# A feed-forward's second matrix by Strassen's method for the latent tokens, with the context's products after them

## The reference

```python
def _ffn_sublayer(x, shift, scale, gate, w13, w2, g, b):
    a = _modulate(x, shift, scale) @ w13               # w13: 1024 x 5632, w2: 2816 x 1024
    y = (silu(a[..., :D_FF]) * a[..., D_FF:]) @ w2
    return _layer_norm(ALPHA * x + 0.5 * gate * y, g, b)

mod = silu(c) @ w_ada + b_ada                          # nine rows of 1024, for latent and context
x_lat = _ffn_sublayer(x_lat, ml[0:3], first weights)
x_ctx = _ffn_sublayer(x_ctx, mc[0:3], first weights)
y_lat = token_mixer(modulated x_lat, modulated x_ctx)  # two-way mLSTM, windowed attention
x_lat = _layer_norm(ALPHA * x_lat + ml[5] * y_lat)
x_lat = _ffn_sublayer(x_lat, ml[6:9], second weights)
```

## Time and profile before

| | |
|---|---|
| times of three runs | 2237.27, 2233.45, 2234.02 us (median 2234.02) |
| the profiled execution | 2234.15 us, of which the span is 2232.0 us |
| mean granted clock of TensorE | 0.993 of full speed |
| busy: PE, VectorE (DVE), ScalarE (ACT), GpSimd (POOL) | 98%, 65%, 38%, 7% of the span |
| transfers | 293 MB, a mean of 131 GB/s |
| chain of waits that ended last | PE 86%, VectorE 7%, ScalarE 3%, issue 2%, DMA 2% |

### The profile page before, as it was taken

How to read it: one execution, slowest core, us unless ns; L and a number is a source line. 1 busy time by engine, 2 the same in 40 slices (tenths; PEclk the granted TensorE clock), 3 DMA queues, 4 the chain that set the end, 5 groups by cost and what they waited for, 6 DMA issues and landing times.

```text
span 2232.0 us, 31733 instructions
## 1 busy us (share of the span) xinstructions
PE 2186.0 (98%) x11907; PEld 1859.5 (83%) x11911; DVE 1440.1 (65%) x2394; ACT 859.1 (38%) x1477; POOL 146.4 (7%) x153
## 2 busy tenths in 40 slices
PE   9999999999999999999999999989999999999997
PEld 6888888888888888799789978878778888887886
DVE  4677776676446355775562265765777777767787
ACT  3622222222233324542444427741633233326444
POOL 0000000000000000250010003520000000000001
PEclk8999999999999999999999999999999999999999
DMA  7144344553274537323230002432243443439772
GB/s 284 41 143 129 113 118 137 155 160 118 70 275 154 191 109 216 104 71 120 78 109 25 20 20 75 126 124 64 81 137 118 137 131 119 147 105 313 279 233 103
DMA packets 237933, 293.06 MB, mean 131 GB/s; under 512 B 16694, under 2 KB 164846, under 8 KB 237806
## 3 DMA queue, kind: packets, MB, share of 16 engines
q1 hardware_dynamic: 226766, 282.81, 40.0%
q10 hardware_dynamic: 11040, 8.52, 1.3%
HBM read 233.48 MB, written 57.80 MB: 131 GB/s over the span
## 4 chain that ended last, share of the span: by engine, by line
PE 86%; DVE 7%; ACT 3%; issue 2%; DMA 2%; POOL 0%; SPq 0%; ACTq 0%; DVEq 0%; POOLq 0%
PE psum L1278 11%; PE psum L1279 11%; PE psum L1280 11%; PE psum L617 4%; PE psum L619 4%; PE psum L618 4%; PE psum L1919 3%; PE psum L1920 3%; PE psum L1921 3%; PE psum L1444 2%; PE psum L2349 2%; PE psum L1445 2%; PE psum L1446 2%; PE psum L2897 2%; PE psum L1298 2%
## 5 line engine op out<-in xcount | busy, mean ns | idle before, releaser
L1278 PE MATMUL psum<-x_mix_h,x_op_h 128*128 128x512 f32 x640 | 249.9, 390 | 3.7 <-DVE v_sum L1098 3.7
L1279 PE MATMUL psum<-x_mix_l,x_op_h 128*128 128x512 f32 x640 | 249.5, 390 | 0.0
L1280 PE MATMUL psum<-x_mix_h,x_op_l 128*128 128x512 f32 x640 | 249.0, 389 | 0.0
L983 ACT ACTIVATE x_op_h<-raw 128x512 fp32r<-128x512 f32 x140 | 85.9, 627 | 207.3 <-PE psum L1280 121.9
L983 ACT ACTIVATE x_op_h<-w_sum 128x512 fp32r<-128x512 f32 x160 | 97.2, 624 | 160.5 <-DVE w_sum L961 96.0
L1278 PEld LDWEIGHTS psum<-x_mix_h,x_op_h 128*128 128x128 f32 x640 | 120.3, 188 | 28.4 <-DVE x_op_l L989 2.8
L1280 PEld LDWEIGHTS psum<-x_mix_h,x_op_l 128*128 128x128 f32 x640 | 120.2, 188 | 25.3
L1279 PEld LDWEIGHTS psum<-x_mix_l,x_op_h 128*128 128x128 f32 x640 | 120.3, 188 | 23.4
L1444 PE MATMUL psum<-s_high 128*128 128x512 f32 x308 | 120.4, 391 | 3.5 <-DVE s_low L1431 3.4
L1445 PE MATMUL psum<-s_low,s_high 128*128 128x512 f32 x308 | 119.9, 389 | 0.0
L1446 PE MATMUL psum<-s_high,s_low 128*128 128x512 f32 x308 | 119.8, 389 | 0.0
(11 more groups left out here) (411 smaller groups left out, 5702.3 us busy)
## 6 DMA issues: line engine op xcount, KB each, us to landing
raw<-in_ffn_w SPq DMA_DIRECT2D x154, 512.0 KB, 5.1
ada_slice<-in_w_ada SPq DMA_DIRECT2D x56, 512.0 KB, 3.7
f_terms<-g_half SPq DMA_DIRECT2D x77, 256.0 KB, 2.1
s_raw<-f_terms SPq DMA_DIRECT2D x77, 256.0 KB, 3.4
s_raw<-in_ffn_w SPq DMA_DIRECT2D x77, 256.0 KB, 4.1
f_rows<-g_out SPq DMA_DIRECT2D x44, 256.0 KB, 2.7
p_raw<-in_w_in SPq DMA_DIRECT2D x22, 512.0 KB, 5.1
early<-in_w_ada SPq DMA_DIRECT2D x16, 512.0 KB, 7.2
```

Source lines behind the costliest of these rows:

```text
L983: nc.scalar.activation(op_tiles(F, op)[0][:], OP_SOURCE[op], ACT.Copy).then_inc(F.hi, 1)
L1278: nc.tensor.matmul(o, wh[:, k], high(k), start=i < 4 and k == 0, stop=False, skip_group_check=i > 3)
L1279: nc.tensor.matmul(o, wh[:, k], low(k), start=False, stop=False, skip_group_check=i > 3)
L1280: last = nc.tensor.matmul(o, wl[:, k], high(k), start=False, stop=k == KH - 1, skip_group_check=i > 3)
```

## The change

1. The first feed-forward's gated rows become g_half1 as in the second: term stores to DRAM (`term_sp`), and the rows of the context stored alone (`ctx_store`). The four sums of halves of a pair are made by GpSimd (`quick1_pool`). Blocks 0 and 1 gate the odd block's halves in PSUM banks 7 and 6, and ScalarE copies them (`first_halves_act`).
2. The second matrix of the first feed-forward runs through the class `Second` (S1, 77 steps) for the latent tokens. Then come 11 pairs for the two tiles of the context (`c_loads_sp`, `c_high`, `c_low`, `c_unit`, `c_pe`, `c_evacuate_dve`), in banks 4 to 7, with the turns of latent tokens 512 to 1023 behind the first four pairs. The gate rows move into the last quick block.
3. `T2`'s order is latent tokens 512 to 1023, 0 to 511, context. The first 14 projection groups are kv for tiles 4 to 7, o for tiles 4 to 7, kv for 0 to 3, kv for the context, o for 0 to 3. GpSimd's x1 rows go in the order 4 to 7, 0 to 3.
4. The residual rows of the latent tokens are loaded behind pieces 16 to 23, those of the context after the last split of its weights. The rope loads move behind the first of these two.
5. The modulation slices have 512 columns: 112 of 256 KB, turned in 20 groups of four.

`second_loads`, `second_high`, `second_low`, `second_unit`, `second_pe`, `evacuate_dve`, `store_rows`, `plain_stored` and `quick_stored` are gone. Two lists of waits for a free place in the ring (`ring_free1`, `ring_free2`) and counts of what S1 has used before are passed to `Second`; the second feed-forward's order of work stays the same.

The core of the diff (lines of removed functions that are printed above, and buffer places, are left out):

```diff
+        def term_rest_pool(pool, F, pair):
+            e1, e2, o1, o2 = F.half
+            made = 4 * (pair + F.terms_before)
+            gated_in_place(pool, F, pair, 1, 1)
+            pool.wait_ge(term_made, made + 1)
+            nc.gpsimd.tensor_tensor(e2, e2, o2, ALU.add).then_inc(term_made, 1)
+            term_kept(pool, F, pair, 0, 2)
+            nc.gpsimd.tensor_tensor(e1, o2, e1, ALU.subtract).then_inc(term_made, 1)
+            pool.wait_ge(term_made, made + 3)
+            term_kept(pool, F, pair, 2, 1)
+            nc.gpsimd.tensor_tensor(o1, o1, e1, ALU.subtract).then_inc(term_made, 1)
...
+        def c_loads_sp(sp, S, f):
+            F, r = S.F, C_RAW[f]
...
+            if f < 4:
+                sp.wait_ge(F.y_added, 24)
+            else:
+                sp.wait_ge(F.lo, c_item(F, f - 4, 1) + 1)
+            sp.dma_start(c_raw[r][:], w2_view[F.which][f * P:(f + 1) * P, :]).then_inc(step_in[r], 16)
+            sp.dma_start(c_rows[f % 4][:], F.rows[f * P:(f + 1) * P, :]).then_inc(step_in[r], 16)
+        def c_high(act, S, p):
...
+            if p < 2:
+                act.wait_ge(F.lo, S.split(STEPS2 - 1))
+                act.wait_ge(F.y_added, 24)
+            elif p < 4:
+                act.wait_ge(F.y_ready, 4 * len(TERMS))
+            else:
+                act.wait_ge(F.pair_done, C_PARTS + max(i for i in range(p) if C_W2[i] == C_W2[p]) + 1)
+            if p >= 2:
+                act.wait_ge(F.pair_done, C_PARTS + p - 1)
...
+                c_in_place(act, S, f)
+                nc.scalar.activation(c_w2[C_W2[p]][0][:, i], c_raw[C_RAW[f]][:], ACT.Copy).then_inc(F.hi, 1)
...
+                h, l = [g[p % 2][:, i, t * P:(t + 1) * P] for g in (c_g_h, c_g_l)]
+                first, last = p == 0 and i == 0, p == PAIRS - 1 and i == 1
+                nc.tensor.matmul(o, h, wh[:, i, cols], start=first, stop=False)
+                nc.tensor.matmul(o, h, wl[:, i, cols], start=False, stop=False)
+                done = nc.tensor.matmul(o, l, wh[:, i, cols], start=False, stop=last)
...
+        def c_pe(pe, F, after_pair):
+            for p in range(PAIRS):
+                pe.wait_ge(F.lo, c_item(F, 2 * p + 1, 1) + 1)
+                if p == 0:
+                    pe.wait_ge(F.y_read, 12)
+                for u in range(4):
+                    done = c_unit(pe, p, u)
+                    if p == PAIRS - 1:
+                        done.then_inc(F.y_ready, 1)
+                if p < PAIRS - 1:
+                    done.then_inc(F.pair_done, 1)
+                after_pair(p)
...
+        SLICE_PLAN = [[2 * s + i for s in plan for i in range(2)] for plan in SLICE_PLAN]
+        MOD_UNITS = [(g, h, v) for g in range(MODS_LATE) for h in range(2) for v in range(VECTORS[g])]
         def slices_at(j, place):
-            return SLICE_PLAN[j][place:place + 1 if place < 2 else None]
...
+        def first_halves_act(act):
+            act.wait_ge(F1.glu_ready, F1.items.index((1, 1)) + 1)
+            act.wait_ge(F1.ab_ready, 2 * F1.n)
+            for n in range(2):
+                nc.scalar.activation(F1.half[2 + n], psum[:, 7 - n, :], ACT.Copy).then_inc(first_quarter, 1)
...
         def quick1_sp(sp):
...
             slice_sp(sp, 1)
             loaded = 2
             for j in range(QUICK):
+                pair, odd = j // 2 + 1, j % 2
                 if j < QUICK - 1:
                     quick_weights(sp, F, j)
+                if odd:
+                    term_sp(sp, F, pair, "S3")
                 else:
-                    second_loads(sp, F, 0)
-                if j:
-                    quick_stored(sp, F, j - 1, 1)
+                    for term in ("A22", "S1", "S2", "S4"):
+                        term_sp(sp, F, pair - 1, term)
                 if j == QUICK - 1:
-                    second_loads(sp, F, 1)
+                    for s in range(4):
+                        pieces_sp(sp, S1, s)
                 ahead = sum(len(p) for p in SLICE_PLAN[:j + 1])
-                for s in range(loaded, min(ahead + 1, len(SLICES))):
+                for s in range(loaded, ahead):
                     slice_sp(sp, s)
-                    loaded = s + 1
-                quick_stored(sp, F, j, 0)
-                quick_stored(sp, F, j, 2)
+                loaded = max(loaded, ahead)
+                term_sp(sp, F, pair, "A12" if odd else "A11")
+                ctx_store(sp, F, j + 2)
                 for s in range(loaded, min(ahead + 2, len(SLICES))):
                     slice_sp(sp, s)
                     loaded = s + 1
-            quick_stored(sp, F, QUICK - 1, 1)
+            for term in ("A22", "S1", "S2", "S4"):
+                term_sp(sp, F, PAIRS - 1, term)
...
+        def quick1_pool(pool):
+            term_first_pool(pool, F1, 0)
+            for pair in range(PAIRS - 1):
+                term_rest_pool(pool, F1, pair)
+                term_first_pool(pool, F1, pair + 1)
+            term_rest_pool(pool, F1, PAIRS - 1)
...
+        def second1_sp(sp):
+            S, F = S1, F1
+            for s in range(4, STEPS2):
+                pieces_sp(sp, S, s)
+                if 5 <= s < 5 + PAIRS:
+                    kept_sp(sp, S, s - 5)
+                if 16 <= s < 16 + TL:
+                    sp.dma_start(y[:, s - 16, :], token_rows(s - 16)).then_inc(rows_back, 16)
+            for f in range(FB):
+                c_loads_sp(sp, S, f)
+                if f == 17:
+                    kv_loads_sp(sp)
+            sp.wait_ge(F.lo, c_item(F, FB - 1, 1) + 1)
+            sp.dma_start(y[:, TL, :], token_rows(TL)).then_inc(rows_back, 16)
+            rope_loads_sp(sp)
+            piece_load(sp, 2)
+            piece_load(sp, 3)
+            sp.wait_ge(F.pair_done, C_PARTS + PAIRS - 1)
+            sp.dma_start(y[:, TL + 1, :], token_rows(TL + 1)).then_inc(rows_back, 16)
...
+            c_high(act, S, 0)
+            c_high(act, S, 1)
+            for i in range(4, TL):
+                norm_act(act, N1, i, ROWS1[i])
+            for p in range(2, PAIRS):
+                if p == PAIRS - 1:
+                    proj_high(act, 0)
+                    gates_high(act)
+                c_high(act, S, p)
+                if 2 <= p < 6:
+                    turned1_act(act, (2 * p - 4, 2 * p - 3))
+            proj_high(act, 1)
+            norm_act(act, N1, 8, ROWS1[8])
+            norm_act(act, N1, 9, ROWS1[9])
...
+                add_part_dve(dve, S, 2, t)
+            c_low(dve, S, 0)
+            for t in range(4):
+                gate_part_dve(dve, S, 3, t)
+                add_part_dve(dve, S, 3, t)
+                dve.wait_ge(F.y_added, 36 + t + 1)
+                norm_sums_dve(dve, N1, 4 + t, ROWS1[4 + t])
+                if t == 1:
+                    c_low(dve, S, 1)
+            for p in range(2, PAIRS):
+                if p == PAIRS - 1:
+                    proj_low(dve, 0)
+                    gates_low(dve)
+                c_low(dve, S, p)
+                if p == 2:
+                    dve.wait_ge(F.pair_done, C_PARTS + 2)
+                if 2 <= p < 6:
+                    turned1_dve(dve, (2 * p - 4, 2 * p - 3))
+            dve.wait_ge(rows_back, 16 * TA)
+            for t in range(TC):
+                c_evacuate_dve(dve, F, t)
+            norm_sums_dve(dve, N1, TL, ROWS1[TL])
+            proj_low(dve, 1)
+            norm_sums_dve(dve, N1, TL + 1, ROWS1[TL + 1])
...
                     pe.wait_ge(N1.gates_kept, 4)
-                if u >= 2:
-                    pe.wait_ge(F1.y_read, u - 1)
...
+            def after_pair(p):
+                if p == 0:
+                    pe.wait_ge(F.y_read, C_READ)
+                if p < 4:
+                    for k in (2 * p, 2 * p + 1):
                         turn_pe(pe, T2, T2_BANKS, normed, (0, k))
-            second_pe(pe, F1, 0, first_free, gates)
-            second_pe(pe, F1, 1, second_free)
-            second_pe(pe, F1, 2, third_free, after_unit=turned)
-            for k in range(2):
-                turn_pe(pe, T2, T2_BANKS, normed, (1, k))
+            strassen_pe(pe, S, first_free)
...
-            out = rows(0, (TL, TL + 1, 0, 1, 2, 3)) + rows(1, range(4)) + rows(0, range(4, TL)) + rows(1, range(4, TL))
+            out = rows(0, range(4, TL)) + rows(1, range(4, TL)) + rows(0, range(4)) + rows(0, range(TL, TA)) + rows(1, range(4))
...
+        T2_BEFORE = {1: [(1, 0)], 2: [(1, 1)], 3: [(1, 2), (1, 3)], 4: [(1, 4)], 5: [(1, 5)], 6: [(1, 6)], 7: [(1, 7)],
+                     8: [(2, 0), (2, 1)], 9: [(2, 2), (2, 3)], 10: [(2, 4), (2, 5)], 11: [(2, 6), (2, 7)]}
+        T2_CHUNK = [1] * 4 + [0] * 4 + [2] * 2
...
         def kv_loads_sp(sp):
-            sp.wait_ge(F1.ab_ready, F1.products)
...
             sp.dma_start(gate_bias, b_gates[0:1, :].to_broadcast([P, 16])).then_inc(gate_in, 16)
-            wait_pair(sp, F1, 0)
+        def rope_loads_sp(sp):
+            sp.wait_ge(F1.lo, c_item(F1, FB - 1, 0) + 1)
             for t in range(TL):
```

(50 more changed lines are left out.)

616 lines of the change are left out of this document (286 added, 330 removed).

## The result

The kernel after takes 2238.46 us (median of 11 runs, 2235.46 to 2241.63) where before takes 2234.02 in the same runs: a ratio of 1.0022 with a 95% interval of 1.0014 to 1.0030. It is 0.2% slower; the forecast was 2232.1, a hair faster. The measured time lies inside the 2225 to 2240 that the forecast gave its own case, but on the side to which it gave a chance of 0.06 (0.27 for slower by any road). The profiled execution took 2239.72 us, 1.3 above the median; its span is 2237.5.

The account below looks back on a forecast made before the run. The prediction took PE, busy 98% of the span, as the bound. From 2234.15 us, +4.2 for the blocks, -23.6 for the second matrix's stage (132 fewer matmuls included) and +17.3 for the junction gave 2232.1 us; whole range 2209 to 2247.

Parts of the forecast that it names:

- its own case: Whole kernel: the saving is nearly all given back, 2232.1 us, own range 2225 to 2240; chance 0.42.
- stage of the second matrix: First feed-forward's second matrix, Strassen steps, context and gate rows: 283.4 us against 307.0, so -23.6, bounds -28 and -15.
- junction: From the last context product to the end of the first 14 projection groups: +17.3 us, bounds +3 and +25.
- rest: The part behind the fourteenth projection group; no change forecast, 0.
- Section 4: Junction: a late row load, late VectorE and GpSimd's x1 work blocking VectorE make it end at E+74; +17.3 us.
- Section 2: Blocks of the first matrix: GpSimd's 44 sums delay VectorE, mostly hidden in slack; +4.2 us, bounds 0 and 15.
- the late row: Junction's start: the last row tile lands at E+4.4, the context's evacuation waits for it, and PE stands 5 us.
- 1.5 for a clock that falls in the waits: Junction's end: 1.5 us added because PE's clock falls in the waits, giving E+74; mean clock near 0.9.
- VectorE's work too, in halves: Blocks of the first matrix: VectorE's work on the modulation slices stays the same, only in halves; no cost.
- Rival C: Blocks: GpSimd's three sums reach PE before v_sum's sixth product in every even block; 15 us, total 2243; chance 0.22.
- the fifth piece's wait: Start of the Strassen steps: the fifth piece is issued 2.3 us later as GpSimd makes three sums; +2.3 us.
- Rival B: Junction stays cheap, groups take 57 to 62 us, as VectorE gets in between GpSimd's operations; total 2216; chance 0.33.

Follow-up runs that it names:

- run 6: The kernel after, with the four sums of gated halves of each pair made by VectorE in the quick blocks, none by GpSimd; ratio 1.0008 to the kernel before.
- run 7: The kernel after, with each of the twenty modulation transposes one place later in its block; ratio 0.9998 to the kernel before.
- run 8: The kernel after, with the edits of run 6 and run 7 together; ratio 0.9994 to the kernel before.
- run 1: The kernel after, with GpSimd's x1 multiplications and additions cut to 8 columns, a measurement and no usable version; ratio 0.9953 to the kernel before.
- run 5: The kernel after, with the last row tile of y loaded ahead of the rope tables and two weight pieces; ratio 1.0002 to the kernel before.

## Why the prediction was wrong, by its own steps

The forecast's sum was -2.1 us, the medians differ by +4.4. Against the mean of the two profiles on each side (the gate rows, 3.6 us, are counted with the stage as in the forecast):

| part | before | after | difference | forecast |
|---|---|---|---|---|
| up to the stage | 621.3, 618.05 | 630.1, 628.3 | 9.5 - 3.6 = +5.9 | +4.2 |
| stage of the second matrix | 307.0, 307.0 | 280.1, 279.8 | -27.0 + 3.6 = -23.4 | -23.6 |
| junction | 56.6, 53.3 | 75.6, 74.2 | +19.9 | +17.3 |
| rest | 1247.1, 1252.2 | 1251.7, 1251.4 | +1.9 | 0 |
| sum | | | +4.3 | -2.1 |

**The mechanisms came as forecast; the terms that stand for them were too small, and all on one side.** Two steps failed. Section 4, the junction, measured +19.9 where the forecast had +17.3: 2.6 of the 6.4 us. Section 2, the blocks, measured +5.9 where it had +4.2: 1.7, with the narrower slices put at nothing. The other 1.9, in the rest, is no effect that the runs show (below).

**Junction (+17.3, measured +19.9).** A part of the miss lies on each side of the difference.

On the side of the change (E is the last context product, as in the forecast), the junction took 75.6 and 74.2 us, and 75.0, 75.0 and 75.5 in runs 6, 7 and 8, which don't edit it, where the forecast had 74 (its own terms, 70, 3.1 and 1.5, make 74.6). About one microsecond is missing, and the rest of the agreement is partly luck: the late row cost 6.25 and not 5; ln_rows took 8.8 us from issue to landing and not 5.3, so that GpSimd started at E+26.2 and not E+22.7; but by then 10 of VectorE's 36 operations with both inputs in SBUF were through and not 4, and behind GpSimd's run 6 were left and not 13. The "1.5 for a clock that falls in the waits" was too little too: the mean clock is 0.82 and 0.88 in the two profiles, not near 0.9, since not only the first long wait is followed by matmuls at half clock (the last columns: PEclk, DMA share, GB/s):

```profile
916.00:920.00 4.00, 3.36 (x15) 3.36 (x16) 3.86 (x6) 0.00 (x0) 0.00 (x0) 0.50 0.02 4
955.00:960.00 5.00, 2.16 (x10) 2.16 (x11) 4.97 (x3) 1.13 (x2) 5.00 (x2) 0.50 0.10 30
970.00:975.00 5.00, 4.98 (x28) 4.99 (x29) 4.90 (x9) 2.58 (x6) 5.00 (x2) 0.66 0.00 0
980.00:985.00 5.00, 5.00 (x27) 4.96 (x28) 2.24 (x12) 0.54 (x2) 0.00 (x0) 0.66 0.01 3
```

For this PE is busy 58.6 and 55.1 us and not the 50.0 of a clean stretch. Most of it falls where PE would have waited for VectorE: the second profile has 3.6 us less of it and is 1.4 shorter. At the end it is on the path: the last 4.0 us have no gap, at a mean clock of 0.69.

On the side of before, 56.7 us held 3.4 of clock that the second profile of before doesn't have (53.3 us at full clock). So the base was a single sample on its high side, by 1.8 us against the mean of two. What takes the place of the 17.3 is read from run 1: GpSimd's x1 work is worth 17 to 18 us of the 75, and the late row is most of what is left above the matmuls.

**Blocks (+4.2, measured +5.9).** The place was right, transposes that wait for slices of the same place, but PE waits 2.1, 2.1 and 1.2 us there in place of 1.3, 1.3 and 0.5; that is 5.4 us, and 4.7 more than before, where the forecast had 3.1. GpSimd's share was not the mistake: without its sums (run 6) 2.3 us of the 5.4 stay, so 3.1 went with them. The 1.6 us left above before's 0.7 fit the term that section 2 put at nothing, "VectorE's work too, in halves": the same slices in halves cost VectorE some 17 us more (last section). That is argued and not shown apart, since run 6 also gives VectorE 44 sums more. Three sums in a row cost VectorE 2.9 us in four slice operations (5.84 less 4 x 0.745), inside the range given:

```profile
167.45 5.84 DVE L758 SCALAR_TENSOR_TENSOR ada_sums<-ada_slice,more,ada_sums 128x512 f32<-128x512 f32 x4
```

The first quick block waits 3.4 and 2.0 us in the two profiles, 1.8 and 1.6 before, 1.0 more in the mean (forecast 1.1). **Rival C** was right in sign and wrong in its place: with the transposes moved (run 7), PE waits 0.9 us for v_sum outside the first quick block, so GpSimd's sums do find VectorE's slack: a loss of 2.9 us against a slack of 2.8. The rival's price went by a loss of 4.3 us a block, for which the prediction has no row and which lies above its own 2.5 to 3.8. Putting them on VectorE gains nothing (runs 6 and 8).

**Stage (-23.6, measured -23.4).** The Strassen steps were forecast at 215.7 and took 216.5, the fifth piece's wait at 3.9 (1.6 + 2.3) and took 3.84, the context 64.1 and took 63.6.

**Rest (0, measured +1.9).** The two profiles of before differ by 5.1 us among themselves. Seven profiles of the change that have the same instructions in this part (its own two and runs 1, 5, 6, 7 and 8) took 1247.5 to 1251.7 us, 1250.2 in the mean, against 1249.7 for the two of before. So no effect of the change there can be seen, and the forecast's 0 stands. How the blocks and the junction share what is left is uncertain by about as much as the two profiles of before differ, 3.3 us in each.

**Rival B**, the cheap junction, got a third of the chance for the median of 0.69 us among the splits. Ten of those sixteen splits lay outside GpSimd's operations; beside them, the rows of the same group said one operation at a time, and that is what a longer run brings.

## What to carry to other kernels

Where two engines exclude each other, price a stretch by how many operations of the one get through beside how many of the other (here 20 beside 16, and ten beside ten where nothing but such operations stood in line), and not by a median over all of them. A small job that "runs on a free engine" belongs where its neighbour is idle too: sixteen operations cost 17 to 18 us of the junction on GpSimd, half of their gain was lost again when they came a little later, and on VectorE, at the right place, they cost nothing that could be seen. A forecast within a few microseconds of zero needs two profiles or more of the kernel before: one stretch of the same instructions differed by 5 us, and two others by 3.

## What the runs showed of the hardware that was not expected

GpSimd holds up an operation of VectorE with a single tensor in SBUF too; it is seen for one kind, which multiplies 512 columns by one factor per partition. The same 20 instructions without GpSimd's sums (run 8; run 6 has the same 0.48 us) and with them (after), in ns:

```profile
L763 DVE TENSOR_SCALAR ada_sums<-ada_slice,more x20: 477/480/486, 118.7 to 530.5; 128x512 f32<-128x512 f32 x20
```

```profile
L763 DVE TENSOR_SCALAR ada_sums<-ada_slice,more x20: 474/1510/1521, 114.0 to 529.3; 128x512 f32<-128x512 f32 x20
```

The Trainium skill's page "SBUF — State Buffer" (Who interferes with whom) says that such a copy or scaling, in the mode that uses both of VectorE's port pairs, takes the shared pair as well. The rows agree that it is held up; which mode the instructions ran in no row shows. GpSimd's sums of 512 columns are longer beside VectorE too, 1.6 to 1.7 us (medians of two of its lines) and not the 1.27 of the earlier trace rows.

Slices of half the width are dearer: 140 multiply-adds of 512 columns at 0.745 us are 104 us of VectorE, where before's 70 of 1024 at 1.278 are 89. The 20 multiplications above, at 0.48, are 9.6 us where before's ten of 1024 at 0.751 are 7.5.

```profile
L758 DVE SCALAR_TENSOR_TENSOR ada_sums<-ada_slice,more,ada_sums x140: 737/745/1786, 115.5 to 551.4; 128x512 f32<-128x512 f32 x140
```
